# Attention scores as two half-array matmuls per query block in place of one with zero-padded queries

## The reference

```python
q = rmsnorm(q.reshape(B, S, N_HEADS, 2, HEAD_DIM), q_norm_g[l])
k = rmsnorm(k.reshape(B, S, N_HEADS, 2, HEAD_DIM), k_norm_g[l])
...
s = jnp.einsum('bqhcd,bkhcd->bhcqk', qi, k) * scale      # c: component, d: 64
s = s - slopes * dist;  s = where(causal, s, -inf)
p = jax.nn.softmax(s, axis=-1)
a = p[:, :, 0] - lam * p[:, :, 1]
o = jnp.einsum('bhqk,bkhv->bqhv', a, v)
```

## Time and profile before

| | |
|---|---|
| median of 3 runs | 1639.56 us (1634.87 to 1643.62) |
| the profiled execution | 1633.25 us; spans of its cores 1622.2 to 1631.7 us |
| core that the profile shows (the slowest) | core 5, 1631.7 us from first to last instruction |
| granted TensorE clock, mean of a core | 0.995 to 0.999 |
| exps of attention | 640, the first at 351.8 us |
| matmuls | 12112, of them 2208 of 256 columns (2176 scores) and 4352 of 129 (V product) |
| DMA | 186.47 MB, 114 GB/s on average |

### The profile page before, as it was taken

One profiled execution on the slowest core, in us unless ns is written; L12 is line 12 of the kernel. 1 busy time (PEld: TensorE's weight loads), 2 busy tenths in 40 slices (PEclk: granted clock), 3 DMA queues, 4 the chain that ended last, 5 costly groups with the idle time before them and its releaser, 6 DMA issues.

```text
span 1631.7 us, 33211 instructions; the slowest of 8 cores (1622.2 to 1631.7 us)
## 1 busy us (share of the span) xinstructions
PE 1543.4 (95%) x12112; PEld 952.2 (58%) x12112; DVE 639.8 (39%) x1161; ACT 989.5 (61%) x1398; POOL 66.7 (4%) x109
## 2 busy tenths in 40 slices
PE   5899999989999899999999999989999999999999
PEld 2455555558888687777777776644444444444444
DVE  3565555541353533313313334565452251341321
ACT  5777777769999798888798886832141140230220
POOL 0000000000000000000100001001100000000000
PEclk9999999999999999999999999999999999999999
DMA  9446666326645542434652125475480211302002
GB/s 286 121 121 144 154 143 162 104 50 156 130 103 120 117 119 51 98 79 107 173 130 92 40 74 196 152 247 173 142 277 27 91 40 52 103 1 78 27 20 72
DMA packets 65262, 186.47 MB, mean 114 GB/s; under 512 B 23040, under 2 KB 23680, under 8 KB 62720
## 3 DMA queue, kind: packets, MB, share of 16 engines
q1 hardware_dynamic: 60272, 154.86, 30.8%
q0 software_dynamic: 4832, 29.50, 9.7%
HBM read 178.17 MB, written 48.37 MB: 139 GB/s over the span
## 4 chain that ended last, share of the span: by engine, by line
PE 77%; ACT 9%; DMA 6%; issue 4%; DVE 4%; SPq 0%; ACTq 0%; DVEq 0%; POOL 0%; POOLq 0%
PE psum L173 77%; ACT arena L173 9%; DVE arena L173 4%; DMA arena<-w_gc 2%; DMA arena<-xkv 1%; DMA arena<-wch 1%; DMA arena<-w_uc 1%; DMA wch<-arena 1%; DMA arena<-wub 0%; SPq L173 0%; ACTq L163 0%; DVEq L163 0%; POOL arena L173 0%; SPq L163 0%; POOLq L163 0%
## 5 line engine op out<-in xcount | busy, mean ns | idle before, releaser
L173 PE MATMUL psum<-arena 128*128 128x129 bf16 (+3 forms) x12112 | 1543.4, 287 | 84.9 <-DVE arena L173 49.8
L173 PEld LDWEIGHTS psum<-arena 128*128 128x128 bf16 x12112 | 952.2, 98 | 675.7 <-issue 155.4
L173 ACT ACTIVATE arena<-psum,arena 128x1024 bf16<-128x1024 f32 (+4 forms) x708 | 643.9, 958 | 147.1 <-PE psum L173 135.0
L173 ACT ACTIVATE arena<-psum 128x512 bf16<-128x512 f32 (+1 forms) x292 | 167.0, 595 | 375.7 <-PE psum L173 350.2
L173 DVE SCALAR_TENSOR_TENSOR arena<-psum,arena 128x512 bf16<-128x512 f32 (+1 forms) x240 | 169.0, 710 | 247.9 <-ACT arena L173 160.3
L173 ACT ACTIVATE arena<-arena 128x1 f32<-128x1 f32 (+4 forms) x314 | 172.6, 563 | 60.3 <-DMA arena<-xkv 22.3
L173 DVE TENSOR_TENSOR arena<-arena 128x512 bf16<-128x512 f32 (+6 forms) x213 | 142.8, 687 | 106.9 <-DMA arena<-w_gc 36.1
L173 DVE COPY arena<-psum 128x1024 bf16<-128x1024 bf16 (+5 forms) x162 | 97.2, 603 | 152.1 <-PE psum L173 149.8
L173 DVE SCALAR_TENSOR_TENSOR arena<-arena,psum 128x512 f32<-128x512 f32 x64 | 43.7, 687 | 191.5 <-PE psum L173 160.0
L173 DVE TENSOR_TENSOR arena<-psum,arena 128x512 f32<-128x512 f32 x32 | 22.1, 692 | 196.0 <-PE psum L173 196.0
L173 DVE TENSOR_SCALAR arena<-arena 128x1024 bf16<-128x1024 f32 (+4 forms) x123 | 61.3, 501 | 39.2 <-ACT arena L173 33.5
(11 more groups left out here) (9 smaller groups left out, 10.8 us busy)
## 6 DMA issues: line engine op xcount, KB each, us to landing
arena<-xkv SPq DMA_DIRECT2D x64, 512.0 KB, 5.2
arena<-wch SPq DMA_DIRECT2D x32, 768.0 KB, 4.9
w_b<-w POOLq DMA_DIRECT2D x32, 512.0 KB, 6.3
arena<-w_b SPq DMA_DIRECT2D x32, 512.0 KB, 10.0
arena<-x1s SPq DMA_DIRECT2D x32, 512.0 KB, 4.5
arena<-w_gc SPq DMA_DIRECT2D x16, 512.0 KB, 5.6
arena<-xkv SPq DMA_DIRECT2D x32, 256.0 KB, 4.7
x1s<-arena POOLq DMA_DIRECT2D x32, 256.0 KB, 3.2
```

The source lines that it names most:

```text
L173: return lambda e: getattr(e, name)(*a, **k)
```

## The change

The two components' scores of a block become two matmuls that contract over 64 partitions each: component 0 with the upper half of K's tile and of `QT[s]`, component 1 with the lower half. Component c writes bank 2 * sp + c, with block i at columns 128 * i, where before both components of a block lay side by side in bank 2 * sp + i // 2. A built program gives such a matmul 64 x 128 of the array, at row 0 or at row 64. `PT` is laid out by component and then block, so the exp of a partial step covers two strips, and `emit_pv` and the exp take other columns. `Qz`, `zero_qz` and `make_qz` go. As `QT[0]` is now read until the last step, `load_g2t` moves behind attention.

```diff
-        o_Qz = [T0 + 45184, T0 + 47232]
...
-        def make_qz(idx, s, h):
-            k = idx % 2
-            for c in range(2):
-                pr = slice(64 * c, 64 * c + 64)
-                P.emit("dve", I("tensor_copy", out=Qz[k][pr, :, 128 * c:128 * c + 128],
-                                in_=QT[s][pr, h, :].rearrange("p (i t) -> p i t", t=128)),
-                       reads=[t_Q[s]], writes=[t_Qz[k]])
...
-                A[5] = both(A[5], zero_qz)
-                A[6] = both(A[6], lambda: make_qz(0, 3, 0))
...
-            qz = Qz[idx % 2]
             for i in range(i0, 4):
                 g = 4 * s + i - d
-                bi = 2 * sp + i // 2
-                P.emit("pe", I("matmul", bank(bi)[:, 256 * (i % 2):256 * (i % 2) + 256], lhsT=KTg[g][:, h, r * 128:(r + 1) * 128],
-                               rhs=qz[:, i, :], start=True, stop=True),
-                       reads=[t_KT[g], t_Qz[idx % 2]], writes=[tb[bi]])
+                for c in range(2):
+                    bi = 2 * sp + c
+                    pr = slice(64 * c, 64 * c + 64)
+                    P.emit("pe", I("matmul", bank(bi)[:, 128 * i:128 * i + 128], lhsT=KTg[g][pr, h, r * 128:(r + 1) * 128],
+                                   rhs=QT[s][pr, h, i * 128:(i + 1) * 128], start=True, stop=True),
+                           reads=[t_KT[g], t_Q[s]], writes=[tb[bi]])
...
-            c0 = 256 * i0
+            c0 = 128 * i0
...
-            rd = [tb[2 * sp + 1]] + ([tb[2 * sp]] if i0 < 2 else [])
+            rd = [tb[2 * sp], tb[2 * sp + 1]]
+            pin = psum[:, 1024 * sp:1024 * (sp + 1)]
+            pout = PT[pt]
+            if c0:
+                pin = pin.rearrange("p (c t) -> p c t", c=2)[:, :, c0:512]
+                pout = pout.rearrange("p (c t) -> p c t", c=2)[:, :, c0:512]
...
-            P.emit("act", I("activation", out=PT[pt][:, c0:1024], in_=psum[:, 1024 * sp + c0:1024 * (sp + 1)],
+            P.emit("act", I("activation", out=pout, in_=pin,
...
-                    P.emit("pe", I("matmul", ob, lhsT=PT[pt][:, a * 128:(a + 1) * 128], rhs=Vg[g][:, r, h * VS:h * VS + 129],
+                    P.emit("pe", I("matmul", ob, lhsT=PT[pt][:, (c * 4 + i) * 128:(c * 4 + i + 1) * 128], rhs=Vg[g][:, r, h * VS:h * VS + 129],
...
-                at(starts[idx] + 3, lambda idx=idx: make_qz(idx + 1, *order[idx + 1]))
...
-        at(starts[15] + 2, load_g2t)
...
-        sched = {1: [LD2[1]], 13: [NA2[0], lambda: fnq.append(LD2[2])], 17: [NA2[1], lambda: fnq.append(LD2[3])]}
+        sched = {1: [load_g2t, LD2[1]], 13: [NA2[0], lambda: fnq.append(LD2[2])], 17: [NA2[1], lambda: fnq.append(LD2[3])]}
```

More of the change, by code:

```diff
@@ L1247, in build_nc @@
             at(e, lambda idx=idx: fin1(idx))
-            if idx + 1 < len(order):
-                at(starts[idx] + 3, lambda idx=idx: make_qz(idx + 1, *order[idx + 1]))
             at(e, lambda idx=idx, s=s, h=h: fnq.extend(head_end(idx, s, h)))
```

## The result

| | before | changed |
|---|---|---|
| median of 7 runs | 1638.17 us | 1651.77 us |
| ratio to before, undisturbed runs | | 1.0084 (95%: 1.0062 to 1.0106) |
| profiled execution; longest span | 1633.25 us; 1631.7 us (core 5) | 1646.70 us; 1645.2 us (core 4) |
| matmuls | 12112 | 14288 |

The medians are of all runs, the ratio leaves out the disturbed ones of both kernels. The change makes the kernel 0.8% slower, where 1601 us, 2.3% faster, was forecast.

A forecast was written before the change was run, and what follows sets the result against it. PE was taken to pace steps with fillers, ACT the others. Savings of 9.6, 17.7, 8.3 and 2.7 us in stages 3 to 0 made 38.3 off 1633.25, 1595.0, or 1601 us on the runs' scale; range 1582 to 1735.

The forecast's parts named there:

- What bounds the kernel: Attention: PE paces the 353 steps with fillers, ACT the 287 without, at 1.007 us for a full step.
- The pair of scores: Scores, per query block: two half-array matmuls take 60 ns in place of one of 109, saving 49 ns.
- The seam: Each change between full-array and half-array matmuls, two a step: 30 ns taken, between ends of 0 and 194.
- 60 ns a step: Cost taken for a step's two changes between full-array and half-array matmuls, 30 ns each.
- the sum's own terms: Steps with fillers: 49 ns saved a block, 60 ns paid a step; stage 2: 540 x 49 - 146 x 60 = 17.7 us.
- the seams drain the array: Rival, at each step's two changes of form: up to 194 ns each, +94 us, 1734 us; 110 to 194 given 0.30.
- the turn at 98 ns a seam: Full steps: price per change of form at which two of them eat the 196 ns saved.
- Zero-padded queries: Before the scores: 32 copies and two memsets leave DVE, 39% busy; counted as 0, at most 9 us.
- Exp over two strips: The 192 exps of partial steps on ACT: two strips cost 0 more; far end 50 us, given no weight.
- The range: Whole kernel: 1582 to 1735 us, said to hold nearly all the cases as priced.
- seams near the turn: Case for the changes of form in each step: 60 to 110 ns each, 1618 to 1653 us, chance 0.13.
- the likeliest case: Changes of form at 0 to 60 ns each with overlapping halves: 1583 to 1618 us, chance 0.43.

The follow-up runs named there:

- x_split: Changed kernel with each step's scores and V product interleaved in halves, four changes of form a step instead of two, same matmuls; 1751.1 us, ratio 1.0727.
- x_quiet: Changed kernel with the sixteen casts of w_1 begun at step 66 instead of step 10; 1640.3 us, ratio 1.0032.
- b_quiet: Kernel before with the sixteen casts of w_1 begun at step 66 instead of step 10; 1637.6 us, ratio 1.0018.
- x_full: Changed kernel with every score matmul full-array, 128 rows by 128 columns over zero-padded queries, so no change of form; 1646.5 us, ratio 1.0074.
- x_hybrid_quiet: Changed kernel with half-array pairs only in full steps, full-array scores over zero-padded queries in partial ones, w_1 casts from step 66; 1636.95 us, ratio 1.0011.
- x_pair4_quiet: Changed kernel with two steps' scores emitted together, a fourth PT tile, and w_1 casts from step 66; 1666.3 us, ratio 1.0216.

## Why the prediction was wrong

- *What bounds the kernel: right.* In the heads without pauses the steps without fillers kept ACT's pace: the second head of stage 3 took 64.4 us, before 64.8. Steps with fillers are PE's, as 1.53 us in x_split shows.
- *The pair of scores: right, and a little cautious.* Taken at 60 ns with ends of 56 and 112, measured 57. Of the two readings of the weight loads the trace's held: they don't stand in the way of the halves. By the rule of the Trainium skill's page "TensorE: Matmul & The Clock Gate", section "The mechanism", as I applied it, a pair would have cost 86 ns; the runs give 57.
- *The seam: this is the step that failed.* The term "60 ns a step" for two changes of form was mis-sized: they cost 212 ns, 106 each, against ends of 0 and 194. I took the lowest price that a restart had shown (30 ns, from the start of a load to the start of its matmul) and left out the wait ahead of the load. That wait is what the traces show: the load at a seam starts 92 ns after the filler before it has streamed, and the matmul 4 ns later. With 106 ns the sum's own terms give, in stage 2, 540 x 52 - 146 x 212 = 28.1 - 31.0 = -2.9 us; the stage lost 1.4 to 1.6. In a full step it is nearly even: 4 x (109 - 57) = 208 saved, 212 paid. Over all four stages the same terms make some 8 us lost of the 38.3 saved, that is 46 of the 52 us between the gain of 38.3 that I forecast and the loss of some 14 that was measured. The rival "the seams drain the array" named place and direction, and the turn at 98 ns a seam; its price of 194 ns was too high. The rule of the Trainium skill's page "TensorEngine Tiling (Array Packing)", section "Key Properties", that a change of the tiling mode drains TensorE agrees with these runs in that every change costs time, 106 ns, a number that it doesn't give. That the array is empty by then isn't shown: the first score starts 312 ns after a filler whose modelled end is 379 ns after its start.
- *Left out altogether: PE's instruction supply.* I counted columns and loads, not instructions. With 2176 more matmuls and their loads the changed kernel has 4.2 to 10.6 us of pauses per core in stage 3, and lower clocks behind them. With most of them gone (x_quiet) it is at 1.0032, and stage 3 is at 265.1 us on the mean of the cores in place of 271.9. So they are the larger part of the measured loss, though not of the forecast's miss.
- *Zero-padded queries: nearly right.* I counted 0. DVE's timeline before attention in the kernel before:

```profile
346.57 0.91 DVE L173 MEMSET arena<- 128x1024 bf16 x1 [0.16 <-issue]
347.65 0.91 DVE L173 MEMSET arena<- 128x1024 bf16 x1 [0.16 <-DVE arena L173]
348.48 0.63 DVE L173 CAST arena<-psum 128x512 bf16<-128x512 f32 x1
...
349.25 2.76 PE L173 MATMUL psum<-arena 128*128 128x512 bf16 x16 [1.78 <-DVE arena L173]
```

The two memsets stood ahead of a cast on which PE waited for 1.78 us. The change gains this, at most 2 us; I had counted it as nothing, because the engine is 39% busy. The other profiles bear it out: on the mean of the cores attention starts at 348.4 to 349.7 us in the four kernels that have the memsets (before, b_quiet, x_full, x_hybrid_quiet), and at 345.8 to 347.9 in the changed kernel, x_quiet, x_split and the two with four PT tiles.
- *Exp over two strips: right.* An exp of 768 columns takes 902 ns in the changed kernel and 901 before, one of 256 takes 473 and 475; in x_hybrid_quiet the strips remain and stage 2 is as short as before.
- *The range* held the result (1651.8 in 1582 to 1735), and the case "seams near the turn", 1618 to 1653, held it too at 0.13. In part that is luck: the seam does lie in that case's 60 to 110 ns, but some 8 us of stage 3 come with pauses that no case had a term for. The chance for slower was 0.42. The fault was to let the likeliest case rest on the smallest price in sight.

Open: by what path the casts delay a fetch; why x_hybrid_quiet and x_pair4_quiet pause in spite of their later place; and whether the lower clock after a pause would be there with the fetches on time.

## What to carry to other kernels

Half-array matmuls in pairs do run in the time of one, but each change between them and full-array ones costs some 106 ns here, so count seams first: a block of pairs pays only if it saves more than two seams (by these numbers, an estimate that no run tried, five pairs of this size or more), and bringing blocks together to save seams must not serialize what two sets of banks kept apart. Count instructions as well as columns. Where the change adds many small matmuls, look for pauses of PE without a semaphore and for a record of the instruction queue just before each ends.

## What was not expected of the hardware

- A seam is about half of what waiting for the last matmul's end would cost: 106 ns against the 194 that I had worked out from the modelled 220 ns of the earlier trace rows.
- PE can stand still for up to 6.0 us at a time (one core of the changed kernel) with no semaphore to wait for, at 32 instructions a microsecond; in the changed kernel a later place for sixteen DRAM-to-DRAM casts, on a queue of another engine, takes most of that away, in two variants of it not.
- The granted clock fell to 0.91 on average over such a head (72 us with 8.2 us of pauses), and its lower level lasted into the work after a pause, where a 129-column matmul took 107 ns in place of 57.
